# A hybrid encoder block on eight cores: norm chains in half steps, tokens in two groups of four, the residual kept in its slots, and a ring of weights that starts at other offsets

## The reference, cut to what matters

```python
def rms_norm(x, gain): ...                     # x * rsqrt(mean(x*x) + EPS) * gain
    h = rms_norm(x, g_pre_mix[i])
    proj = h @ w_in[i]                         # conv branch, GLA branch, two merge gates
    ...
    mix = sigmoid(gate_a) * y_a + sigmoid(gate_b) * y_b
    x = x + rms_norm(mix @ w_mix_out[i], g_post_mix[i])
    h = rms_norm(x, g_pre_ffn[i])
    f = (silu(h @ w_ff_gate[i]) * (h @ w_ff_up[i])) @ w_ff_down[i]
    x = x + rms_norm(f, g_post_ffn[i])
    h = rms_norm(x, g_pre_ple[i])
    e = sigmoid(h @ w_ple_gate[i]) * (p[i] @ w_ple_proj[i])
    x = x + rms_norm(e, g_post_ple[i])
```

## Time and profile before

| what | value |
|---|---|
| time, median of 3 runs | 2484.18 us (2246.94 to 2606.28) |
| time of the profiled execution | 2248.31 us |
| span of its slowest core, core 6 | 2246.7 us |
| spans of all cores | 2229.5 to 2246.7 us |
| mean granted TensorE clock of all cores | 0.955 to 0.964 |
| PE, DVE, ACT busy | 2024.7, 608.3, 461.2 us |

### The profile page before, as it was taken

The page is one execution under the profiler, slowest core; times in us unless marked ns, Lnnn a source line. Parts: engine busy times, 40 slices in busy tenths (PEclk is TensorE's granted clock), DMA queues, the critical chain, the costliest instruction groups (busy, mean ns, idle before and its releaser), DMA issues.

```text
span 2246.7 us, 25355 instructions; the slowest of 8 cores (2229.5 to 2246.7 us)
## 1 busy us (share of the span) xinstructions
PE 2024.7 (90%) x9746; PEld 938.1 (42%) x9936; DVE 608.3 (27%) x891; ACT 461.2 (21%) x989; POOL 74.0 (3%) x105
## 2 busy tenths in 40 slices
PE   2889888899999999998799999999999999963895
PEld 1344334444444444444344444444444444431342
DVE  3562554443311212114600000011000000034335
ACT  2463444310011111123200000000000000022236
POOL 0000000000000000000000000000000000000000
PEclk9999899999999999998999999999999999976897
DMA  7154030544344344357554444444435444478517
GB/s 199 57 131 76 13 63 1 85 95 77 65 85 78 65 83 85 73 91 176 167 94 75 76 77 79 79 78 79 78 59 101 78 78 78 78 203 195 137 28 243
DMA packets 50435, 210.98 MB, mean 94 GB/s; under 512 B 3307, under 2 KB 4715, under 8 KB 41740
## 3 DMA queue, kind: packets, MB, share of 16 engines
q0 software_dynamic: 38608, 137.44, 35.9%
q1 hardware_dynamic: 11708, 71.90, 9.5%
HBM read 321.59 MB, written 25.17 MB: 154 GB/s over the span
## 4 chain that ended last, share of the span: by engine, by line
PE 79%; DVE 7%; DMA 5%; ACT 5%; issue 4%; DVEq 0%; SPq 0%; ACTq 0%; POOL 0%; POOLq 0%
PE bank L356 78%; ACT arena L344 4%; DVE arena L350 3%; DMA arena<-x1s 2%; DVE arena L347 2%; DMA arena<-w_v 1%; DMA arena<-xp 1%; PE bank L364 1%; DVE arena L410 1%; DMA arena<-p 1%; ACT L344 1%; DVE arena L496 1%; DVEq L157 0%; SPq L377 0%; ACTq L157 0%
## 5 line engine op out<-in xcount | busy, mean ns | idle before, releaser
L356 PE MATMUL bank<-arena 128*128 128x512 bf16 (+2 forms) x9090 | 1972.4, 375 | 56.4 <-DVE arena L347 16.3
L356 PEld LDWEIGHTS bank<-arena 128*128 128x128 bf16 (+2 forms) x9280 | 892.6, 99 | 1120.1 <-issue 117.9
L347 DVE TENSOR_TENSOR arena<-bank,arena 128x512 f32<-128x512 f32 (+4 forms) x432 | 315.3, 739 | 1394.1 <-PE bank L356 888.3
L344 ACT ACTIVATE arena<-bank 128x512 f32<-128x512 f32 (+7 forms) x400 | 223.6, 561 | 1458.3 <-PE bank L356 1431.5
L344 ACT ACTIVATE arena<-arena 128x1 f32<-128x1 f32 (+4 forms) x392 | 196.2, 508 | 262.8 <-DVE arena L350 157.1
L364 PE MATMUL bank<-arena 128*128 128x128 bf16 x656 | 59.2, 247 | 139.0 <-DVE arena L410 76.3
L364 PEld LDWEIGHTS bank<-arena 128*128 128x128 bf16 x656 | 47.3, 110 | 161.4 <-issue 159.1
L350 DVE SCALAR_TENSOR_TENSOR arena<-arena 128x512 f32<-128x512 f32 (+1 forms) x56 | 80.4, 1436 | 39.2 <-ACT arena L344 18.4
L347 DVE TENSOR_TENSOR arena<-arena 128x512 f32<-128x512 f32 (+3 forms) x144 | 75.5, 529 | 14.6 <-DVE arena L347 1.2
L410 DVE TENSOR_SCALAR arena<-arena 128x2048 bf16<-128x2048 f32 x32 | 41.0, 1281 | 48.6 <-ACT arena L344 48.6
L332 POOL DMA_DIRECT2D arena<-w_ffu x44 | 31.0, 705 | 613.2 <-PE bank L356 599.0
(11 more groups left out here) (25 smaller groups left out, 28.2 us busy)
## 6 DMA issues: line engine op xcount, KB each, us to landing
arena<-w_ffu POOLq DMA_DIRECT2D x44, 1024.0 KB, 9.0
arena<-w_gate POOLq DMA_DIRECT2D x16, 1536.0 KB, 12.7
arena<-w_fd POOLq DMA_DIRECT2D x16, 1408.0 KB, 11.7
arena<-x SPq DMA_DIRECT2D x16, 1024.0 KB, 6.5
arena<-w_conv POOLq DMA_DIRECT2D x8, 1536.0 KB, 13.1
arena<-xp SPq DMA_DIRECT2D x8, 1024.0 KB, 6.8
arena<-w_mix POOLq DMA_DIRECT2D x4, 2048.0 KB, 16.2
x1s<-arena SPq DMA_DIRECT2D x8, 1024.0 KB, 11.6
```

Source lines behind the costliest of these rows:

```text
L344: P.emit("act", lambda e: e.activation(out=out, in_=in_, func=func, **kw), reads=reads, writes=writes, partw=partw)
L347: P.emit("dve", lambda e: e.tensor_tensor(out=out, in0=in0, in1=in1, op=op), reads=reads, writes=writes, partw=partw)
L356: P.emit("pe", lambda e, l=l, r=r, j=j: e.matmul(out_ap, lhsT=l, rhs=r, start=(start and j == 0), stop=(stop and j == n - 1)), reads=reads ...
```

## The change

From the mix stage on, all regions are placed by hand (`take_at`), and the code is written in another order.

- **Ring.** `ring["at"] = 16384` is set before the first `w_mix`, and `ring["at"] = 0` before the first `w_fd`. The third `w_ple` goes through the ring, and so does the fourth.
- **Mix.** The last two column blocks run for tiles 0 to 3, then for tiles 4 to 7: (2, 0-3), (3, 0-3), (2, 4-7), (3, 4-7). Both `w_mix` loads are held until the end.
- **Norm chain.** `Post.one(j)` does rstd and add of tile j, and Square, Ln, Exp and scale (now a Copy with a scale on ACT instead of the product on DVE) of tile j-1. `Post.two(j)` does the flip of tile j-2. `paced` assigns both to numbered steps. In the first chain `one(j)` is at step 2j and `two(j)` at 2j+1; steps 0 to 11 follow mix blocks, 12 to 19 the half blocks of the first four up passes.
- **Embeddings.** `p` is loaded and transposed during up passes 8 to 16.
- **Second chain.** Steps 0 to 11 follow the down blocks from (part 3, tiles 0-3) on, the steps from 12 on follow `ple_block`s. The residual is loaded from `x1s` into eight slots `X` as space comes free, is added there and stays; `x2s` is gone.
- **Embedding gate.** Column blocks 0 and 1 run as (0, 0-3), (1, 0-3), (0, 4-7), (1, 4-7). In blocks 0, 1 and 3 the Sigmoid is made of Exp, Ln, Exp on ACT. `ple_part(2, ...)` is called after the first two column blocks, `ple_part(3, ...)` after the third.
- **Last pass.** The gate's result stays in one of two slots `tl[q]`; it is multiplied by the gain in place, and `finish(i-1)`, two DVE adds (1536 and 512 columns) into `X`, stands behind the products of tile i.

```diff
+        def one(self, j):
...
+                rstd_ops(st, stb[j], D)
+                r2 = st[:, 2:3]
+                for out, m, x, rds, wr in self.parts(j):
+                    stt(out, m, r2, x, ALU.mult, ALU.add, [stb[j]] + rds, wr)
...
+                self.after_add(j)
+            if 1 <= j <= 8:
+                i = j - 1
...
+                norm_stat(i, t, tb, xn, xnb)
+                act(xn, t, AF.Copy, [tb, stb[i]], [xnb], scale=stats[:, i, 2:3])
+
+        def two(self, j):
+            if 2 <= j <= 9:
+                i = j - 2
+                norm_ev(norm_tp(self.pool, self.xn[i % 2], self.xnb[i % 2]), self.gi, self.hTn[i], self.hTnb[i])
...
+    todo = paced(post, {j: 2 * j for j in range(9)}, {j: 2 * j + 1 for j in range(2, 10)})
...
+    ring["at"] = 16384
+    mixw = {}
+    for cbk, tiles in ((0, range(8)), (1, range(8)), (2, range(4)), (3, range(4)), (2, range(4, 8)), (3, range(4, 8))):
+        if cbk not in mixw:
+            flat, wb = wload(w_mix[cbk])
+            mixw[cbk] = (k3(flat, 16), wb)
...
     while every.n % 8:
         every.next()
+    ring["at"] = 0
...
+            todo = paced(post, {0: 0, 1: 3, 2: 6, 3: 9, 4: 11, 5: 13, 6: 15, 7: 17, 8: 19}, {2: 7, 3: 10, 4: 12, 5: 13, 6: 15, 7: 17, 8: 19, 9: 20})
...
+    for s, tiles in ((0, first4), (1, first4), (0, last4), (1, last4)):
+        for i in tiles:
+            ple_block(i, s, False)
+            step()
+    assert not todo, todo
+    ple_part(2, 0, 18)
     for i in range(8):
...
+        ple_block(i, 2, True)
+    ple_part(3, 0, 18)
     for i in range(8):
...
+        bp, bbp, bg, bbg = ple_mm(i, 3)
+        q = n_e["n"] % 2
+        n_e["n"] += 1
+        sg, sb_ = tl[q], tlb[q]
+        late[i] = (sg, sb_)
+        gate(sg, sb_, bg, bbg, False)
+        if i > 0:
+            rstd_of(i - 1)
+        tt(sg, bp[:, :], sg, ALU.mult, [bbp, sb_], [sb_])
+        act(jk, sg, AF.Square, [sb_], [jkb], [ssqpb[i]], accum_out=ssqp[:, i, 3:4])
+        tt(sg, sg, gbs_r[3].ap, ALU.mult, [sb_, gbs_b[3]], [sb_])
+        if i > 0:
+            finish(i - 1)
```

More of the change, by code:

```diff
@@ L1016, in take_hid, with ff_up @@
             hidb.append(bs)
-    take_hid(4)
-    sg_r = [M.take(2048, F32) for _ in range(2)]
+    take_hid(0, 4)
+    sg_r = [at(151552 + 2048 * j, 2048) for j in range(2)]
     sgb2 = [r.buf(f"sgf{j}") for j, r in enumerate(sg_r)]
     sg_n = {"n": 0}
-    def ff_up(w, wb, fc, half):
+    def ff_up(w, wb, fc, half, between=None):
         wg, wu = k3(w[:, 0:2048], 16), k3(w[:, 2048:4096], 16)
@@ L1031, in ff_up @@
         act(sg_r[q].ap, bg[:, :], AF.Silu, [bbg], [sgb2[q]])
+        if between is not None:
+            between()
         bu, bbu = every.next()
@@ L1034, in ff_up, with embed, embed_flip @@
         tt(hid[fc][:, ts], bu[:, :], sg_r[q].ap, ALU.mult, [bbu, sgb2[q]], partw=[hidb[fc][half]])
+        if between is not None:
+            between()
     first = []
[L1037 removed]
     for fc in range(4):
         first.append(wload(w_ffu[fc]))
[L1040 to L1042 removed]
+        ff_up(*first[fc], fc, 0, step)
+    for n in sorted(todo):
+        for f in todo[n]:
+            f()
     for fc in range(4):
         ff_up(*first[fc], fc, 1)
[L1045 to L1049 removed]
+    M.drop(*m_r, *xs_r, *xn_r)
+    for lo, n in ((8192, 7), (22528, 11), (45056, 11), (67584, 11)):
+        take_hid(lo, n)
+    pst = [at(131072 + 1024 * j, 1024) for j in range(2)]
+    pstb = [r.buf(f"pst{j}") for j, r in enumerate(pst)]
+    pbf = [at(133120 + 512 * j, 512, BF16) for j in range(2)]
+    pbfb = [r.buf(f"pbf{j}") for j, r in enumerate(pbf)]
+    def embed(i):
+        j = i % 2
+        P.dma("sp", f"ldp{j}", lambda e: e.dma_start(out=pst[j].ap, in_=p_d[i * 128:(i + 1) * 128, :]), writes=[pstb[j]])
+        P.emit("dve", lambda e: e.tensor_copy(out=pbf[j].ap, in_=pst[j].ap), reads=[pstb[j]], writes=[pbfb[j]])
+    def embed_flip(i):
+        j = i % 2
+        bk, bb = every.next()
+        ptv = transposes(bk, bb, [pbf[j].ap[:, 0:128], pbf[j].ap[:, 128:256]], [pbfb[j]])
+        act(pT[:, :, i * 128:(i + 1) * 128], ptv[:, 0:256].rearrange("p (k t) -> p k t", k=2), AF.Copy, [bb], partw=[pTb])
     for fc in range(4, 44):
@@ L1132, in build_program @@
-    for i in range(8):
-        pf, pfb = load_tile(pst, p_d, i * 128)
-        _, pb, pbb = pbf.next()
-        P.emit("dve", lambda e, o=pb, a=pf: e.tensor_copy(out=o, in_=a), reads=[pfb], writes=[pbb])
-        bk, bb = every.next()
-        ptv = transposes(bk, bb, [pb[:, 0:128], pb[:, 128:256]], [pbb])
-        act(pT[:, :, i * 128:(i + 1) * 128], ptv[:, 0:256].rearrange("p (k t) -> p k t", k=2), AF.Copy, [bb], partw=[pTb])
-    ple = {}
-    def ple_part(s, c0, c1, region=None):
-        src = w_ple[s][:, c0 * 512:c1 * 512]
-        if region is None:
-            flat, wb = wload(src)
-        else:
-            flat, wb = region.ap, wfixed(region, f"ple{s}", src)
+            take_X(1, 0)
@@ L1147, in ple_part @@
+        if (part, tiles) == (2, last4):
+            M.drop(hid_r[3])
+            take_X(4, 45056)
+            take_X(5, 53248)
+            take_hT3(2, 61440)
+    M.drop(hid_r[4])
+    take_X(6, 65536)
+    take_X(7, 73728)
+    take_hT3(3, 81920)
+    take_hT3(7, 86016)
+    ple = {}
+    def ple_part(s, c0, c1):
+        flat, wb = wload(w_ple[s][:, c0 * 512:c1 * 512])
         w = k3(flat, c1 - c0)
@@ L1155, in build_program, with ple_mm @@
     ple_part(1, 7, 18)
-    sgd_r = [M.take(2048, F32, top=True) for _ in range(2)]
-    sgdb = [r.buf(f"sgd{j}") for j, r in enumerate(sgd_r)]
-    gb3_r, gb3b = load_gb(2)
-    jk3_r = M.take(1024, BF16, top=True)
-    jk3b = jk3_r.buf("jk3")
-    e_r, eb = {}, {}
+    gain(2, 3)
     n_e = {"n": 0}
-    def ple_block(i, s):
+    late = {}
+    def ple_mm(i, s):
         cols, wb = ple[s]
```

310 lines of the change are left out of this document (155 added, 155 removed).

## The result

The change made the kernel slower by 1.3%: the ratio to the kernel before is 1.0127, with a 95% interval of 1.0084 to 1.0171. The runs on which it rests took 2274.8 and 2275.9 us, against 2246.7 and 2246.9. Executions in which a whole die was granted a lower clock are left out of every comparison here, and from `copy_late` to `all_four` so are those of the kernel before in which two or four cores were granted 0.934 to 0.949 (2272 to 2279 us, where its others took 2246 to 2251). The profiled execution has a span of 2273.3 us and took 2274.8, where 2250 was forecast. That lies in the range of 2216 to 2284. But the call was "no change", and the direction is beyond the interval.

The account below looks back on a forecast made before the run. The prediction took PE to bound the kernel, except the last pass, set by ACT and DVE. Its terms, +24.2 - 19.9 + 13.9 - 26.0 + 9.8 = +2.0, gave 2250 us, range 2216 to 2284.

Parts of the forecast that it names:

- Part 1: Gates' end: the first `w_mix` is issued only when PE has finished the last gate pass; +24.2 us.
- rival 2: Loads share the DMA engines, so `w_mix`, `w_ple` and `w_fd` land later; 27 us more, 2277 us, chance 0.17.
- Part 2: Mix and up: norm work hides behind two blocks and a flip; 9.5 us lost instead of 29.4, so -19.9.
- The prediction's sign: Between mix and up, PE has no wait over 3 us for a DVE product into bf16.
- The second edge: Flip of tile 7 at the end of half 0 of up pass 4: PE waits about 2.4 us.
- Part 3: Start of down: the first `w_fd` is issued only after the last two up passes it overlaps; +13.9 us.
- Part 4: Second norm chain and embedding blocks: losses of 80.5 us become 54.5, with bank, load and clock waits.
- The first block waits 1.2: First embedding block: PE waits 1.2 us for the second half of the first `w_ple`.
- 5.2 at block 0: Flip behind the first embedding block: PE waits 5.2 us for its bank, ACT being still at tile 3's Copy.
- Part 5: Last pass: each gate waits for a slot the earlier adds read; cycle 6.95 us, pass 67.4 instead of 57.6, +9.8.
- Rival 1: Embedding blocks: PE hardly waits for banks, 37 us of pauses and clock become about 11; 2224 us, chance 0.20.
- Rival 3: Loads for mix, down and last `w_ple` come in time, so their waits fall away; 2196 us, chance 0.08.

Follow-up runs that it names:

- copy_late: Changed kernel with the first norm chain's Copy of a tile one step later, behind the next block's Square; 2275 us, ratio 1.012.
- all_four: Changed kernel with five edits: no ring jump before mix, last `w_ple` split, later Copy, four last-pass slots, flip banks in turn; 2182 us, ratio 0.9705.
- x_behind: Changed kernel with the first three tiles of x and the mix gains loaded only after the first `w_mix` has landed; 2268.5 us, ratio 1.008.
- mix_slot: Changed kernel without the ring's jump to 16384 ahead of the first `w_mix`; 2239 us, ratio 0.9947.
- fd_slot: Changed kernel without the ring's reset to 0 ahead of the first `w_fd`; 2248 us, ratio 0.9988.
- x4_behind: Changed kernel with residual reloads of tiles 4 to 7 waiting for the first `w_ple`'s second half; 2278 us, ratio 1.0124.
- flip_banks: Changed kernel with the second chain's flips taking banks in turn with the blocks; 2260 us, ratio 1.005.
- late_slots: Changed kernel with four slots instead of two for the last pass's gate result; 2264 us, ratio 1.007.

## Why the forecast of no change was wrong

**Part 1, the gates' end: right in its mechanism, too small.** "The first `w_mix`" was forecast at 22 to land, 22.3 of wait; PE waited 26.9 (26.1 to 28.0 over the cores). The step was "19.6 plus 2.4, the same addition again for the rest". `x_behind` measures it: 16.7 in the mean of the cores without the tiles and gains, and 10.1 more with them, where this step had added 5.7. That is rival 2, at about half of what it asked over the forecast (4.6 of 8.1). `mix_slot` gives the cause back in full: without the jump there is no such wait.

**Part 2, the mix and its norms: the step that failed.** "Both fit, so PE doesn't wait in the middle" added up DVE's 6.4 and ACT's 6.3 against 7.8 and stopped there. The two sums are about right (6.0 and 6.5 us measured); what is missing is that the engines take turns, since the program's order of a bank's readers and ACT's queue chain them into a ring of 9.46. PE doesn't wait in the middle, as banks in flight cover that; the lag piles up and is paid at the edge, 11.7 instead of 2.8. The prediction's sign, no wait of more than 3 us there, came out false. `copy_late` breaks the ring at one place: cycle 7.80, wait 4.1. That shows the mechanism; the time of the longest core didn't fall with it. This is the largest single miss, 8.9 of the 24.6 by which the sum was off. The second edge (2.3) and the fourth `w_mix` (3.3 against 2.8) were right.

**Part 3, the start of down: right.** 14.2 instead of 12.0; 10.4 to 10.6 on four cores and 14.2 to 14.6 on the others. `fd_slot` takes it away.

**Part 4: right in most rows, wrong at the first block.** Forecast and measured: blocks 18.5 and 17.8 (7.68, 4.18, 4.46, 1.20 and 0.29), the last `w_ple` 15.8 and 15.1, the two flips behind blocks 1 and 5 5.5 and 6.3. "The first block waits 1.2" and "5.2 at block 0" make 6.4; measured were 10.2, and `x4_behind` shows that all but some 1.6 of the sum is ACT's. It is the miss of part 2 again: the queue of ACT was counted at its Copy alone, not at the whole norm work ahead of it. `flip_banks` confirms that the banks made about half of the pauses between the blocks (13.4 of 27.2).

**Part 5, the last pass: right.** The cycle is 7.19 against 6.95, the pass 69.3 against 67.4, and `late_slots` shows that the slot sets it. The Trainium skill (ScalarE: Activation LUTs, What ACT_TABLE_LOAD costs) gives a switch a drain of 1.38 us; by that figure, an estimate, this pass would have come out some 11 us shorter than forecast. It came out 1.9 longer, and no drain shows in the changed kernel: a load of 1.28 starts at 2161.73 and the ACTIVATE behind it at 2163.03.

**The clock.** The forecast had about 2 us after the first `w_mix`, 1.5 in the rest of part 2 and 8 in part 4. At 0.2158 us a matmul, the three rows behind the pauses of the mix and up stage (320, 96 and 32 matmuls) are 2.1, 1.9 and 2.1 too long: 6.1 instead of 3.4. In the second stage 482.3 less 404.3 of PE's work and 63.6 of waits leaves 14.4 instead of 9.9. The forecast's sum had 405.3 of work: it moved the transposes of `p` under the up passes, but left their 1.0 here, and put them at nothing there, where they take 0.11 for each tile, 0.9 in all.

The rest adds up. In mix and up: 4.6 and 0.5 for the first and fourth `w_mix`, 8.9 for the first edge, 2.7 for the clock, 0.9 for `p`, 17.6 of the 17.8. In the second stage: 2.2 for `w_fd`, 3.8 for the first block, 4.5 for the clock, -1.0 for `p` and -0.9 for the others, together the 8.6.

**The rivals.** Rival 1 (PE hardly waits for banks) is out: the waits were there, and but for the first block their sums lie within 0.8 us of the forecast's. Rival 2 (loads share the DMA engines) happened at 4.6 and 2.2 us over the forecast, not at 27. Rival 3 (loads in time) is out in this kernel, but `mix_slot` is what it described: 36 us less, where I had put 38 on the two loads of parts 1 and 3. The forecast's sum of +2.0 was a difference of terms of 10 to 26 us. An error of 9 us in one and 4 to 5 in others, nearly all the same way, was enough to take it out of the forecast's own range of 2238 to 2264, which was drawn too narrow for that.

## What to carry to other kernels

When norm work is to hide behind matmuls, don't add up each engine's time: follow one cycle through both queues, since a product behind a Square of the same bank, behind the previous tile's Copy, makes one ring of two engines that are each idle a third of the time. A buffer's address decides when its load may start; at the edge of a stage, print which transfers each first load overlaps before rewriting the order of the work. And when a wait is removed, look at the sum of the next two: here a load that landed 8 us sooner only moved PE's pause to the next instruction.
